# Windowed pooling: division folded into the subtraction, edges scaled first, no tensor of counts

## What is computed

```python
POOL_WINDOWS = (2, 4, 8, 16)
def multiscale_pool(u):
    csum = concatenate([zeros, cumsum(u32, axis=1)], axis=1)
    t = jnp.arange(s)
    for g, w in enumerate(POOL_WINDOWS):
        sl = slice(g * POOL_GROUP_DIM, (g + 1) * POOL_GROUP_DIM)
        lo = jnp.clip(t - w // 2, 0, s - 1)
        hi = jnp.clip(t + w // 2 - 1, 0, s - 1)
        win_sum = jnp.take(cg, hi + 1, axis=1) - jnp.take(cg, lo, axis=1)
        count = (hi - lo + 1).astype(jnp.float32)[None, :, None]
        outs.append(win_sum / count - u32[..., sl])
```

## Time and profile before

| | |
|---|---|
| three runs, us | 1494.47, 1495.72, 1499.38; median 1495.72 |
| the profiled execution, us | 1500.42 |
| its span, first to last instruction, us | 1499.1 |
| mean granted clock of PE | 0.992 |
| PE busy | 98% of the span |
| DVE / ACT / POOL busy | 50% / 58% / 16% |
| memset L1698 | 8 times, 498 ns each |
| multiply L1709 and subtract L1711 | 8 times each, 692 and 693 ns |
| load of the table, issue to landing | 7.7 us |

### The profile page before, as it was taken

One profiled execution on the slowest core, in us unless ns is written; L12 is line 12 of the kernel. 1 busy time (PEld: TensorE's weight loads), 2 busy tenths in 40 slices (PEclk: granted clock), 3 DMA queues, 4 the chain that ended last, 5 costly groups with the idle time before them and its releaser, 6 DMA issues.

```text
span 1499.1 us, 18239 instructions
## 1 busy us (share of the span) xinstructions
PE 1467.2 (98%) x6968; PEld 1195.8 (80%) x6968; DVE 751.7 (50%) x1416; ACT 864.5 (58%) x1153; POOL 246.9 (16%) x272
## 2 busy tenths in 40 slices
PE   9998999999999999999999899999999999999998
PEld 8886888888878788788878777776878888888886
DVE  7889854365595948443134558736663122110011
ACT  7588898745565546554544466587345444444441
POOL 1111111111111111111113421121111111111111
PEclk9999999999999999999999999999999999999999
DMA  9776877899999798798989966885577998888872
GB/s 287 183 186 162 202 194 189 209 304 313 273 251 275 206 220 206 195 261 227 236 211 270 295 165 161 216 250 193 183 196 190 247 224 189 198 193 197 196 183 84
DMA packets 98598, 323.10 MB, mean 216 GB/s; under 512 B 11264, under 2 KB 13568, under 8 KB 98384
## 3 DMA queue, kind: packets, MB, share of 16 engines
q0 software_dynamic: 34160, 124.34, 44.0%
q1 hardware_dynamic: 61104, 191.70, 37.1%
q10 hardware_dynamic: 3248, 5.90, 1.1%
HBM read 178.64 MB, written 17.83 MB: 131 GB/s over the span
## 4 chain that ended last, share of the span: by engine, by line
PE 77%; DVE 9%; DMA 6%; ACT 5%; SPq 2%; issue 1%; POOL 0%; ACTq 0%; DVEq 0%
PE ps L702 24%; PE ps L705 24%; PE ps L703 24%; DMA wlo<-raw 3%; DMA tab<-pl_f 1%; DVE pl_f L1969 1%; DVE pl_r L1544 1%; ACT wlo L1124 1%; ACT whi L1115 1%; DMA pl_f<-pl_f 1%; PE ps L746 1%; DVE pl_f L1667 1%; SPq L2557 1%; PE ps L790 1%; ACT pl_f L1424 1%
## 5 line engine op out<-in xcount | busy, mean ns | idle before, releaser
L702 PE MATMUL ps<-pl_r,whi 128*128 128x512 f32 x1976 | 777.3, 393 | 10.2 <-DMA wlo<-raw 5.0
L705 PE MATMUL ps<-pl_r,whi 128*128 128x512 f32 x1976 | 771.2, 390 | 0.0
L703 PE MATMUL ps<-pl_r,wlo 128*128 128x512 f32 x1976 | 770.8, 390 | 0.0
L702 PEld LDWEIGHTS ps<-pl_r,whi 128*128 128x128 f32 x1976 | 372.0, 188 | 97.0 <-issue 11.9
L705 PEld LDWEIGHTS ps<-pl_r,whi 128*128 128x128 f32 x1976 | 371.8, 188 | 79.3 <-DVE pl_r L1561 0.8
L703 PEld LDWEIGHTS ps<-pl_r,wlo 128*128 128x128 f32 x1976 | 372.0, 188 | 76.0 <-issue 0.5
L2315 POOL DMA_DIRECT2D wlo<-raw x237 | 203.0, 857 | 1127.2 <-ACT wlo L1124 1097.9
L1115 ACT ACTIVATE whi<-raw 128x1024 fp32r<-128x1024 f32 x246 | 259.0, 1053 | 172.0 <-PE ps L705 126.4
L1124 ACT ACTIVATE wlo<-raw 128x1024 fp32r<-128x1024 f32 x237 | 247.8, 1045 | 0.0
L2287 DVE TENSOR_TENSOR pl_f<-ps,pl_f 128x512 f32<-128x512 f32 x22 | 15.2, 691 | 170.6 <-PE ps L705 170.6
L1544 DVE TENSOR_TENSOR pl_r<-pl_f,pl_r 128x512 fp32r<-128x512 f32 x112 | 77.5, 692 | 31.2 <-ACT pl_r L1144 21.7
(11 more groups left out here) (268 smaller groups left out, 1107.0 us busy)
## 6 DMA issues: line engine op xcount, KB each, us to landing
raw<-in_w SPq DMA_DIRECT2D x245, 512.0 KB, 5.5
wlo<-raw POOLq DMA_DIRECT2D x237, 512.0 KB, 6.2
pl_f<-in_mod SPq DMA_DIRECT2D x48, 512.0 KB, 9.1
pl_f<-tab SPq DMA_DIRECT2D x12, 512.0 KB, 7.3
xs<-pl_f SPq DMA_DIRECT2D x16, 256.0 KB, 9.9
tab<-pl_f SPq DMA_DIRECT2D x8, 512.0 KB, 7.2
pl_f<-xs SPq DMA_DIRECT2D x16, 256.0 KB, 7.7
spill<-pl_f ACTq DMA_DIRECT2D x16, 256.0 KB, 4.6
```

The lines of the kernel that those rows point to most:

```text
L702: matmul(out, wh, sr(pair, kk, "hi"), start=start, stop=False)
L703: matmul(out, wl, sr(pair, kk, "hi"), start=False, stop=False)
L705: mm = matmul(out, wh, sr(pair, kk, "lo"), start=False, stop=stop)
```

## The change

The strip is zeroed only in its two margins (w/2 columns on the left, w/2 on the right) by two memsets. The first and last w/2 columns of the window sums are multiplied by w divided by the count, by two small operations from a small table `edge` of 64 numbers per partition. Then one operation over 512 columns multiplies the sums by 1/w and subtracts the token. The table of counts of four slots goes; `edge` holds one slot, and its load is 32 KB.

```diff
@@ layout
-    run([("inv",)], 4)
+    take("edge")
...
-    give("inv")
+    give("edge")
@@ vector_engine, pool
-        memset(f0, 0.0).then_inc(*done.tick(("pl_zero", t)))
+        memset(f0[:, 0:w // 2], 0.0).then_inc(*done.tick())
+        memset(f0[:, w // 2 + S:w + S], 0.0).then_inc(*done.tick(("pl_zero", t)))
         V.wait_ge(at("pl_in", t))
...
-        V.wait_ge(done.now(), at("inv"))
-        tt(prev[:, 0:S], prev[:, 0:S], k.inv[:, t // 2, :], ALU.mult).then_inc(*done.tick())
-        V.wait_ge(done.now())
-        tt(prev[:, 0:S], prev[:, 0:S], f0[:, w // 2:w // 2 + S], ALU.subtract).then_inc(
+        V.wait_ge(done.now(), at("edge"))
+        h = w // 2
+        tt(prev[:, 0:h], prev[:, 0:h], k.edge[:, t // 2, 0, 0:h], ALU.mult).then_inc(*done.tick())
+        tt(prev[:, S - h:S], prev[:, S - h:S], k.edge[:, t // 2, 1, 8 - h:8], ALU.mult).then_inc(
             *done.tick())
-        halves("pooled", t, prev[:, 0:S], ("pl", t), ("inv",))
+        V.wait_ge(done.now())
+        stt(prev[:, 0:S], prev[:, 0:S], 1.0 / w, f0[:, h:h + S], ALU.mult, ALU.subtract).then_inc(
+            *done.tick())
+        halves("pooled", t, prev[:, 0:S], ("pl", t), ("edge",))
@@ sync_engine
-    dma(k.inv, k.inv_d).then_inc(*k.inv_in.tick(("inv",)))
+    dma(k.edge, k.edge_d).then_inc(*k.edge_in.tick(("edge",)))
@@ build
-        k.inv = k.sb("inv").rearrange("p (g n) -> p g n", g=4)
+        k.edge = k.sb("edge")[:, 0:64].rearrange("p (g e n) -> p g e n", g=4, e=2)
@@ lay_out
-    inv = np.zeros((128, 4, S), np.float32)
+    edge = np.ones((128, 4, 2, 8), np.float32)
     for g, wd in enumerate((2, 4, 8, 16)):
...
-        inv[:, g, :] = (1.0 / (hi - lo + 1)).astype(np.float32)
+        share = (wd / (hi - lo + 1)).astype(np.float32)
+        edge[:, g, 0, 0:wd // 2] = share[0:wd // 2]
+        edge[:, g, 1, 8 - wd // 2:8] = share[S - wd // 2:S]
```

More of the change, by code:

```diff
@@ L213, with __init__ @@
 class Kit:
-    def __init__(self, nc, top, x_d, w_d, mod_d, cond_d, vec_d, cst_d, inv_d, ssm_d, uk_d, spill_d,
+    def __init__(self, nc, top, x_d, w_d, mod_d, cond_d, vec_d, cst_d, edge_d, ssm_d, uk_d, spill_d,
                  tab_d, xs_d, out_d):
         self.nc = nc
-        self.x_d, self.w_d, self.mod_d, self.vec_d, self.cst_d, self.inv_d = (
-            x_d, w_d, mod_d, vec_d, cst_d, inv_d)
+        self.x_d, self.w_d, self.mod_d, self.vec_d, self.cst_d, self.edge_d = (
+            x_d, w_d, mod_d, vec_d, cst_d, edge_d)
         self.cond_d, self.xs_d = cond_d, xs_d
@@ L246, in __init__ @@
         self.gain_in, self.raw_part = sig("gain_in", 16), sig("raw_part", 16)
-        self.vec_in, self.ident_in, self.tri_in, self.inv_in = (
-            sig(n, 16) for n in ("vec_in", "ident_in", "tri_in", "inv_in"))
+        self.vec_in, self.ident_in, self.tri_in, self.edge_in = (
+            sig(n, 16) for n in ("vec_in", "ident_in", "tri_in", "edge_in"))
         self.ssm_in, self.uk_in, self.ki_in = (sig(n, 16) for n in ("ssm_in", "uk_in", "ki_in"))
@@ L2762, in lay_out @@
     x = f["x"][0].T.reshape(8, 128, S)
-    arrays = {"x": x, "w": stream, "mod": mod, "cond": cond, "vec": vec, "cst": cst, "inv": inv, "ssm": ssm,
+    arrays = {"x": x, "w": stream, "mod": mod, "cond": cond, "vec": vec, "cst": cst, "edge": edge, "ssm": ssm,
               "uk": uk}
@@ L2768 @@
 SHAPES = {"x": (8, 128, S), "w": (NUNIT, 128, UB * 128), "mod": (48, 128, 1024), "cond": (128, 1024),
-          "vec": (128, NV), "cst": (2, 128, 128), "inv": (128, 4, S), "ssm": (128, 4, 16, 32),
+          "vec": (128, NV), "cst": (2, 128, 128), "edge": (128, 4, 2, 8), "ssm": (128, 4, 16, 32),
           "uk": (128, 2, 512)}
```

## The result

| | before | after |
|---|---|---|
| median of 12 runs each | 1499.57 us (1494.47 to 1504.77) | 1495.54 us (1491.49 to 1497.87) |
| profiled execution, its span | 1500.42, 1499.1 us | 1496.24, 1494.9 us |
| stall and low clock in the mixing stage, 110 to 140 us | 25.66 of 30 busy, clock 0.89 | 28.77 of 30 busy, clock 1.00 |

The ratio after / before is 0.9965, 95% interval 0.9951 to 0.9978: 5.2 us less (3.3 to 7.3), just over the 0.3% that can be told from no change. The two medians in the table lie 4.0 us apart, inside the same interval. Forecast were 4.5 us less, 1491.2 us against the median of the runs then shown; the measured 1495.54 lies inside the range, and nearer its upper end because the kernel before measured 3.9 us higher this time than in the three runs shown.

What follows compares the result with a forecast made beforehand. TensorE was taken as the bound, losing about 8.6 us to stalls and low clock in the mixing stage; 4.5 us would be gained through ACT's earlier weight copies, from the median 1495.72 to 1491.2 us, range 1487.8 to 1496.3.

Steps and rivals of the forecast that it cites:

- R1: Rival, chance 0.12: small DVE operations cost their full length; 0.48 us saved per tile, 2.8 us in all, 1492.9.
- (1): ACT's copy of pooling tile p5 comes 4.30 us sooner; the weight unit behind it only 3.90, bounded by TensorE's buffer.
- (3): At pooling tile p6, 4.16 us is left on ACT; about 0.9 us bank stall remains, TensorE about 7.2 ahead.
- (4): TensorE waits 1.8 us for the copy of weight unit 24, which leaves it 5.3 us ahead.
- (5): ACT's copy of pooling tile p7 comes 4.51 us sooner; TensorE waits again at weight unit 27, starting 4.5 sooner.
- (2): From 81 to 109 us ACT is almost always busy: 3.90 us is carried through, DVE's further saving on p5 lost.
- B: TensorE's stall of 0.69 us at 116.32, waiting for a copy of weight remainders; forecast to go.
- R2: Rival, chance 0.15: weight unit 27's copy lands in 4.4 us, so only unit 24 limits; 5.3 us gained, 1490.4.
- R3: Rival, chance 0.13: another wait of equal length replaces DVE's backlog in the mixing stage; 0 to 1 us gained, 1495.2.
- R4: Rival, chance 0.10: slower, as the layout makes loads on SP's queue and weights behind them late; two stalls give 1501.3.
- C: TensorE's stalls of 1.20 us at 124.61 and 2.46 at 128.02, for a PSUM bank DVE had not read out.
- D: TensorE's stall of 0.39 us at 167.21 in the mixing stage, waiting for a copy of weight remainders.

## Why the prediction was right

**The small operations.** Timeline of DVE of the kernel after, which answers to the earlier trace rows:

```profile
70.09 0.06 DVE L1698 MEMSET pl_f<- 128x4 f32 x1
70.10 0.06 DVE L1699 MEMSET pl_f<- 128x4 f32 x1
...
73.09 0.17 DVE L1711 TENSOR_TENSOR pl_f<-pl_f,pl_f 128x4 f32<-128x4 f32 x1
73.17 0.16 DVE L1712 TENSOR_TENSOR pl_f<-pl_f,pl_f 128x4 f32<-128x4 f32 x1
...
73.36 0.69 DVE L1715 SCALAR_TENSOR_TENSOR pl_f<-pl_f 128x512 f32<-128x512 f32 x1
74.09 0.43 DVE L1550 CAST pl_r<-pl_f 128x512 fp32r<-128x512 f32 x1
```

The memsets cost 0.07 together (70.09 to 70.10 plus 0.06) for the 0.15 I took, so the copy may go some 0.41 us sooner, not 0.35. The passes take 74.09 - 73.09 = 1.00 for 1.46: 0.46 saved, 0.44 forecast. Per tile 0.87 for 0.79, and from copy to copy even 0.89 (5.46 to 4.57 between p3 and p4). R1 is refuted by these rows: small operations without a wait between them overlap (starts 0.01 and 0.08 apart, 0.06 and 0.17 long). What I weighed from the Trainium skill (VectorE: DVE Perf Modes, "The DRAIN you can't avoid") was its general rule; the same section adds that a next operation that is not held starts earlier, and it is this half that the rows show.

**The carrying, step by step.** The profile after is shifted by 2.21 us, the later start of block 32: 0.66 of it stands already at block 16 (20.91 for 20.25), behind the wait of 1.45, and 1.55 comes behind that, with the clock down. With the 2.21 added back, each step can be read. Timeline of ACT after, which answers to the earlier trace rows:

```profile
77.30 0.60 ACT L1218 ACTIVATE pl_f<-ps 128x512 f32<-128x512 f32 x1 [1.64 <-DVE pl_f L1699]
...
79.09 1.07 ACT L1115 ACTIVATE whi<-raw 128x1024 fp32r<-128x1024 f32 x1 [1.19 <-PE ps L705]
...
114.34 0.60 ACT L1218 ACTIVATE pl_f<-ps 128x512 f32<-128x512 f32 x1 [1.04 <-DVE pl_f L1699]
...
117.40 1.05 ACT L1115 ACTIVATE whi<-raw 128x1024 fp32r<-128x1024 f32 x1
...
150.56 0.60 ACT L1218 ACTIVATE pl_f<-ps 128x512 f32<-128x512 f32 x1 [5.42 <-DVE pl_f L1699]
```

and the two copies of weight remainders, which answer to the earlier trace rows:

```profile
142.88 0.85 POOL L2319 DMA_DIRECT2D wlo<-raw  x1 [11.13 <-ACT wlo L1124]
...
DMA to landing us min/median/max: 4.4/4.4/4.4
...
157.25 0.84 POOL L2319 DMA_DIRECT2D wlo<-raw  x1 [3.04 <-ACT wlo L1124]
...
DMA to landing us min/median/max: 7.2/7.2/7.2
```

| step | before | after | sooner, with 2.21 | forecast |
|---|---|---|---|---|
| (1) unit 15, rounding | 80.77 | 79.09 | 3.9 | 3.90 |
| (3) unit 22, rounding | 119.20 | 117.40 | 4.0 | 4.16 |
| (4) unit 24, copy issued | 144.67 | 142.88 | 4.0 | 4.16 |
| (5) p7, ACT's copy | 152.85 | 150.56 | 4.5 | 4.51 |
| (5) unit 27, copy issued | 159.53 | 157.25 | 4.5 | 4.5 |
| (5) unit 27, TensorE | 167.21 | 164.59 | 4.8 | 4.5 |

- (1) The copy of p5 came 5.2 us sooner, for 4.30 forecast, but the unit behind it waits for TensorE to free the buffer (1.19), as forecast: what goes beyond 3.9 is lost.
- (2) DVE waits for ACT at 107.47, now for 2.69 us, and B is gone.
- (3) The bank wait is 1.24, forecast 0.9, and so over the 1 us that was set as a sign; the clock stays at 1.00, forecast so.
- (4) The wait at unit 24 is 1.63, forecast 1.8; the copy took the 4.4 us assumed.
- (5) The wait at unit 27 is 0.55, and the stretch is 4.84 (repeated pair 4.62) shorter, forecast 4.5. The profile names DVE as releaser (its last read of the bank, L1667), but the copy of this unit, issued at 157.25, landed 7.2 later, at 164.45, and the matmul follows 0.14 behind it. What decides is SP's next load, which waits for the same landing and nothing of DVE. After:

```profile
164.47 0.33 SPq L2433 DMA_DIRECT2D raw<-in_w  x1
```

and before:

```profile
166.53 0.75 DVE L1667 SCALAR_TENSOR_TENSOR pl_f<-ps,vec,pl_f 128x511 f32<-128x511 f32 x1
...
167.09 0.33 SPq L2429 DMA_DIRECT2D raw<-in_w  x1
```

The matmul starts 0.12 behind that load both times (164.59, 167.21), and before it starts even ahead of the end of DVE's read (167.28). So the copy releases it, and the bank comes free at nearly the same time. Of the 0.3 us that come out better, 0.3 are the faster landing (7.5 before).
- (6) From 170 to 380 us there is no stall, as forecast.

R2 wanted unit 27's copy in 4.4 us; it took 7.2. R3 wanted 0 to 1 us; the stretch has 4.8. R4's layout and load are nothing in the two runs made for them.

What failed in the prediction is small. The copy of p7 was put "near 148.3" and came at 150.56, and TensorE's waits came some 2 us behind the times given: both because of that later start, which the sum does not hold. The copy of p5 ran 0.9 us further ahead than costed, and the cap behind it hid that. The sign "stalls behind 380 us" says little: they moved by 0.5 us in the first pair and 3.7 in the second, and by 3.4 between the two profiles of before.

How much hung on "no fall of the clock" at C? It was taken from the length of one idle time, and the runs bear it out. But the total did not need it: with the passes alone the clock did fall there, and the stretch was shortened by what ACT's copy of p7 gained (2.21 and 2.04). By the prediction's own steps a fall that costs 2.6 would leave TensorE 4.6 us ahead, and it would still meet unit 27's copy 4.5 ahead (an estimate from its sums). In this stage the low clock cost time only where no wait for ACT's weights followed, as with the margins zeroed ahead. That the 8.6 us at the start are the sum of what TensorE loses is right; that they are "the most that faster pooling can give" hides that the stretch of the kernel before was already set by the copy behind the last and smallest of those waits, D.

## What to carry to other kernels

Where an engine works in program order, look for what stands at the head of its queue and waits for a trivial operation of a busy engine: here a memset held ACT's copy, and the copy held the weights of another stage. Moving that memset a tile ahead gave more (5.9 us) than the removal of work (4.8), and the work removed was worth 0.9 once the order was mended. Before a stall is counted as a loss, look whether a later wait would take it up: at C the low clock cost the stage nothing, because TensorE was held again at unit 27. And ask of every gain what the sped-up engine meets next: two edits that each lost time alone gave 3.9 us together.

## What the runs showed of the hardware that I had not expected

- Two memsets of 4 columns start 0.01 us apart, closer than two small arithmetic operations (0.08).
- TensorE's clock fell from 2.4 to 1.2 GHz in the mixing stage behind waits of 2.55, 2.95 and 3.06 us, and behind one of 2.46 that came three matmuls after a shorter one (1.20 before, 0.43 with the passes alone); it stayed behind 1.63, 1.72 and 2.10. So an edit that turns two short waits into a longer one can lose its gain to the clock. Length alone does not decide: near 22 us, among small matmuls, it fell behind 1.05 and stayed behind 1.30.
- The matmul that directly follows the wait of 2.95 still took 0.47 us, and the fall came behind it; those behind 2.46, 2.55 and 3.06 took 0.79, 0.77 and 0.76. The clock of a window, not the first matmul, tells whether it fell.
